# Seven whole tiles in the ring of expert weights, four turns an expert, and a router in another order

## The reference, cut to what matters

```python
logits = t @ w_router                                # 256 tokens x 8 experts
top_vals, top_idx = lax.top_k(logits, 2)
gates = softmax(top_vals)
for e in range(8):                                   # w_gate, w_up: 1024 x 3584; w_down: 3584 x 1024
    he = (silu(t @ w_gate[e]) * (t @ w_up[e])) @ w_down[e]
    out = out + combine[:, e:e + 1] * he             # combine holds the gates of the chosen experts
...
return rmsnorm(h, final_norm)
```

## Time and profile before

| | us |
|---|---|
| median of 3 runs (2175.14 to 2179.47) | 2176.42 |
| the profiled execution | 2182.77 |
| its span, first to last instruction | 2180.7 |
| TensorE busy | 2114.9 (97%) |
| VectorE, ScalarE, GpSimd busy | 837.9, 465.8, 24.7 |
| moved by DMA | 534.35 MB, mean 245 GB/s |

### The profile page before, as it was taken

How to read it: one execution, slowest core, us unless ns; L and a number is a source line. 1 busy time by engine, 2 the same in 40 slices (tenths; PEclk the granted TensorE clock), 3 DMA queues, 4 the chain that set the end, 5 groups by cost and what they waited for, 6 DMA issues and landing times.

```text
span 2180.7 us, 67375 instructions
## 1 busy us (share of the span) xinstructions
PE 2114.9 (97%) x30418; PEld 1945.7 (89%) x30418; DVE 837.9 (38%) x2085; ACT 465.8 (21%) x1074; POOL 24.7 (1%) x43
## 2 busy tenths in 40 slices
PE   9999999999999999999997899999999999999998
PEld 8889999856999986899986789999999999999997
DVE  4357676314766655467759520101010101010102
ACT  3432112113311134211023221111111111111112
POOL 1000000000000000000000000000000000000000
PEclk9999999999999999999998999999999999999999
DMA  9241444240334423324431338999999999999997
GB/s 394 93 173 72 162 174 175 81 169 8 139 150 169 160 97 136 155 117 174 168 142 40 116 117 327 413 416 410 418 410 418 409 418 409 418 417 416 418 417 287
DMA packets 78407, 534.35 MB, mean 245 GB/s; under 512 B 9106, under 2 KB 9235, under 8 KB 41939
## 3 DMA queue, kind: packets, MB, share of 16 engines
q1 hardware_dynamic: 74450, 519.82, 59.3%
q0 software_dynamic: 3840, 12.85, 1.6%
HBM read 523.00 MB, written 9.63 MB: 244 GB/s over the span
## 4 chain that ended last, share of the span: by engine, by line
PE 65%; DMA 4%; DVE 2%; ACT 1%; issue 1%; DVEq 0%; SPq 0%; ACTq 0%
PE ps L1866 24%; PE ps L1224 12%; PE ps L1882 11%; PE ps L1266 7%; DMA slot<-in_w_moe 4%; PE ps L1141 4%; PE ps L1633 2%; PE ps L1616 1%; DVE scr L2549 0%; PE ps L1813 0%; PE ps L1157 0%; PE ps L1503 0%; PE ps L1489 0%; PE ps L1096 0%; PE ps L1570 0%
## 5 line engine op out<-in xcount | busy, mean ns | idle before, releaser
L1866 PE MATMUL ps<-scr,slot 128*64 128x88 f32 x14336 | 595.4, 241 | 11.1 <-issue 5.4
L1866 PEld LDWEIGHTS ps<-scr,slot 128*64 128x64 f32 x14336 | 562.8, 137 | 22.1 <-issue 12.4
L2698 DVE TENSOR_TENSOR scr<-scr,ps 128x88 f32<-128x88 f32 x224 | 55.1, 246 | 727.1 <-ACT scr L982 727.1
L1882 PE MATMUL ps<-scr,slot 128*64 128x88 f32 x7168 | 315.5, 239 | 1.9 <-issue 1.9
L1882 PEld LDWEIGHTS ps<-scr,slot 128*64 128x64 f32 x7168 | 292.0, 137 | 5.1 <-issue 5.1
L1266 PE MATMUL ps<-scr,slot 128*128 128x256 f32 x1056 | 237.6, 380 | 1.6 <-DVE scr L2369 1.6
L1266 PEld LDWEIGHTS ps<-scr,slot 128*128 128x128 f32 x1056 | 196.6, 191 | 26.0 <-DVE scr L2369 2.0
L982 ACT ACTIVATE scr<-ps 128x88 f32<-128x88 f32 x224 | 54.5, 243 | 743.8 <-PE ps L1866 743.8
L1224 PE MATMUL ps<-vtok,slot 128*128 128x128 f32 x1056 | 139.6, 275 | 0.0
L1224 PEld LDWEIGHTS ps<-vtok,slot 128*128 128x128 f32 x1056 | 128.8, 192 | 0.2
L1224 PE MATMUL ps<-vtok,proj 128*128 128x128 f32 x1056 | 128.7, 275 | 0.0
(11 more groups left out here) (412 smaller groups left out, 2058.4 us busy)
## 6 DMA issues: line engine op xcount, KB each, us to landing
slot<-in_w_moe SPq DMA_DIRECT2D x224, 1024.0 KB, 12.2
slot<-in_w_moe SPq DMA_DIRECT2D x224, 512.0 KB, 12.2
slot<-in_w_ffn SPq DMA_DIRECT2D x33, 3072.0 KB, 10.8
slot<-in_w_even_in SPq DMA_DIRECT2D x3, 3072.0 KB, 27.2
slot<-in_w_odd_qk SPq DMA_DIRECT2D x2, 3072.0 KB, 10.6
slot<-in_w_s_glu SPq DMA_DIRECT2D x2, 3072.0 KB, 11.9
slot<-in_w_odd_v SPq DMA_DIRECT2D x2, 2048.0 KB, 8.4
slot<-in_w_even_in SPq DMA_DIRECT2D x2, 1536.0 KB, 10.6
```

What stands on the lines that cost most here:

```text
L1866: m = pe.matmul(gate_up(j, k)[s:s + STRIP], w[:, o:o + STRIP], xg[:, c], start=c == 0, stop=c == KD - 1, skip_group_check=True)
L1882: m = pe.matmul(y_sum(d)[s:s + STRIP], w[:, o:o + STRIP], hid[j][:, 0:CAP], start=False, stop=False, skip_group_check=True)
L2698: dve.tensor_tensor(hid[f % 4][:, 0:CAP], gbuf[f % 4][:, 0:CAP], gate_up(f, 1), ALU.mult).then_inc(hid_ready, 1)
```

## The change

`RING` becomes 7 and an expert is `TURNS` = 4 turns of seven tiles. The ring takes tiles 0 to 6 as well: places of 12 KB a partition, two to a slot, so three and a half slots. A tile is one transfer of 1.5 MB, issued when its place's last `down` is done; the early issue of the up part is gone. `hrow`, `xl` and `returned` move to other tensors. The seventh tile of a turn has its gate and up sums in bank 6, the others in banks 4 and 5 as before. TensorE's experts 0 to 6 are one loop with their change inside (so `turn_rows` is run once more, on one row loaded in addition), and the last expert has a loop of three turns and one turn written out. `hrow` is made after tiles 7 and 8 and waits for no place. In the router the products for the final gain come after the counts, four products that fill time (`busy`, bank 5) stand in their old place, ScalarE does the exponent of the gates before the two copies, and TensorE waits for those copies at the first change of expert. The branch for crowded experts changes likewise and isn't shown.

```diff
@@ -41,8 +41,9 @@
 UP, DOWN = 2 * D, D
-RING = 4
-GROUPS = FE_TILES // RING
+RING = 7
+TURNS = FE_TILES // RING
+ROUNDS = EXPERTS * TURNS
 WEIGHTED_AT = 16
@@ -262,7 +263,9 @@
 def gate_up(f, k):
-    return ps[:, 4 + f % 2, k * CAP:(k + 1) * CAP]
+    if f % RING == RING - 1:
+        return ps[:, 6, k * CAP:(k + 1) * CAP]
+    return ps[:, 4 + f % RING % 2, k * CAP:(k + 1) * CAP]
 small_loaded, late_loaded = sem("small_loaded"), sem("late_loaded")
@@ -312,8 +315,7 @@
 combined, first_copied = sem("combined"), sem("first_copied")
-moe_up_loaded = [sem(f"moe_up_loaded{i}") for i in range(RING)]
-moe_down_loaded = [sem(f"moe_down_loaded{i}") for i in range(RING)]
+moe_loaded = [sem(f"moe_loaded{i}") for i in range(RING)]
 moe_free = sem("moe_free")
@@ -427,24 +429,16 @@
 mix0 = {"even_out": 0, "odd_out": KD, "mla_o": 2 * KD}
-lead_slots, ring_slots = ([(len(LOADED) - SLOTS + k) % SLOTS for k in some]
-                          for some in ((0, 1), (2, 3)))
-def up_places(two):
-    return [slots[two[h // 3]][:, h % 3 * UP:(h % 3 + 1) * UP] for h in range(RING)]
-def down_places(two):
-    return [slots[two[1]][:, UP + h * DOWN:UP + (h + 1) * DOWN] for h in range(RING)]
-lead_loaded = [_n[k] + 16 * n for k, n in zip(lead_slots, (3, 1 + RING))]
-lead_ups, lead_downs = up_places(lead_slots), down_places(lead_slots)
-ups, downs = up_places(ring_slots), down_places(ring_slots)
-lead = [slots[k] for k in lead_slots]
-hrow = lead[0][:, 0:2 * D].rearrange("p (g d) -> p g d", g=2)
-xl = lead[0][0:CAP, 2 * D:3 * D]
-returned = lead[1][:, 0:4 * D].rearrange("p (n d) -> p n d", n=4)
+tile_slots = [(len(LOADED) - SLOTS + h // 2) % SLOTS for h in range(RING)]
+places = [slots[s][:, h % 2 * (UP + DOWN):(h % 2 + 1) * (UP + DOWN)]
+          for h, s in enumerate(tile_slots)]
+ups, downs = [x[:, 0:UP] for x in places], [x[:, UP:UP + DOWN] for x in places]
+hrow = proj[:, 8:16].rearrange("p a n -> p (a n)").rearrange("p (g d) -> p g d", g=2)
+xl = proj[0:CAP, 16:20].rearrange("p a n -> p (a n)")
+returned = [yT[:, 4:8].rearrange("p a n -> p (a n)"),
+            xbp[:].rearrange("p a n -> p (a n)")[:, 0:D],
+            rgw[:].rearrange("p k j n -> p (k j n)"), part(34, 4)]
 where = part(25)[:, 16:64].rearrange("p (n c) -> p n c", c=8)
@@ -493,43 +487,17 @@
     return SLOTS + max(n for n in range(len(LOADED)) if n % SLOTS == s) + 1
-def load_up(h, unit):
-    sp.dma_start(ups[h], a["w_moe"][bass.ds(unit, 1), :, 0:UP].rearrange(
-                     "o p n -> p (o n)")).then_inc(moe_up_loaded[h], 16)
-def load_down(h, unit):
-    sp.dma_start(downs[h], a["w_moe"][bass.ds(unit, 1), :, UP:UP + DOWN].rearrange(
-                     "o p n -> p (o n)")).then_inc(moe_down_loaded[h], 16)
+def load_tile(h, unit):
+    sp.dma_start(places[h], a["w_moe"][bass.ds(unit, 1), :, :].rearrange(
+                     "o p n -> p (o n)")).then_inc(moe_loaded[h], 16)
 for h in range(RING):
-    for s in lead_slots[0:1 if h < 3 else 2]:
-        sp.wait_ge(slot_free, left(s))
-    sp.dma_start(lead_ups[h], a["w_moe"][h, :, 0:UP]
-                 ).then_inc(slot_loaded[lead_slots[h // 3]], 16)
-for h in range(RING):
-    sp.dma_start(lead_downs[h], a["w_moe"][h, :, UP:UP + DOWN]
-                 ).then_inc(slot_loaded[lead_slots[1]], 16)
-for h in range(RING):
-    for s in ring_slots[0:1 if h < 3 else 2]:
-        sp.wait_ge(slot_free, left(s))
-    load_up(h, RING + h)
-for h in range(RING):
-    load_down(h, RING + h)
-last = EXPERTS * FE_TILES // RING - 1
-sp.wait_ge(up_ready, 2 * (FT0["moe"] + RING) + 2)
-load_up(0, 2 * RING)
-with sp.Fori(2, last) as i:
+    sp.wait_ge(slot_free, left(tile_slots[h]))
+    load_tile(h, h)
+with sp.Fori(1, ROUNDS) as i:
     for h in range(RING):
-        sp.wait_ge(up_ready, i * (2 * RING) + (2 * (FT0["moe"] + h - RING) + 4))
-        load_up((h + 1) % RING, i * RING + (h + 1))
         sp.wait_ge(moe_free, i * RING + h + 1)
-        load_down(h, i * RING + h)
-for h in range(RING):
-    if h + 1 < RING:
-        sp.wait_ge(up_ready, 2 * (FT0["moe"] + (last - 1) * RING + h) + 4)
-        load_up(h + 1, last * RING + h + 1)
-    sp.wait_ge(moe_free, last * RING + h + 1)
-    load_down(h, last * RING + h)
+        load_tile(h, i * RING + h)
 for g in range(2):
@@ -564,11 +532,12 @@
         pool.wait_ge(mo["loaded"], 16 * (e - 2))
-    pool.dma_start(xl, rows_in[e * T:e * T + CAP, :]).then_inc(mo["loaded"], 16)
+    n = CAP if e < EXPERTS else 1
+    at_ = min(e, EXPERTS - 1) * T
+    pool.dma_start(xl[0:n], rows_in[at_:at_ + n, :]).then_inc(mo["loaded"], 16)
 pool.wait_ge(mo["scattered"], ZEROED)
 pool.wait_ge(mo["rows"], 3)
-pool.wait_ge(moe_free, RING + RING)
 for n in range(4):
@@ -584,7 +553,7 @@
     pool.indirect_dma_start(
-        out=returned[:, n], out_offset=None, in_=rows_out,
+        out=returned[n], out_offset=None, in_=rows_out,
         in_offset=bass.IndirectOffsetOnAxis(ap=back_row[:, n:n + 1], axis=0)
@@ -1010,13 +979,13 @@
     take_tokens(1)
+    act.wait_ge(rt["diff"], 2)
+    act.activation(tiny[:, GA:GA + 1, 0:2], tiny[:, GA:GA + 1, 0:2], ACT.Exp
+                   ).then_inc(rt["exp"], 1)
     for b in range(2):
...
                        ).then_inc(fin["rowtaken"], 1)
-    act.wait_ge(rt["diff"], 2)
-    act.activation(tiny[:, GA:GA + 1, 0:2], tiny[:, GA:GA + 1, 0:2], ACT.Exp
-                   ).then_inc(rt["exp"], 1)
 def final_norm():
@@ -1707,12 +1676,7 @@
     pe.wait_ge(tile_taken, TILE0["s5_glu"] + 2 * KD)
-    for c in range(KD):
-        m = pe.matmul(ps[:, 6 + c // 4, c % 4 * P:c % 4 * P + P],
-                      v("final_norm", c).to_broadcast([P, P]), ident, start=True, stop=True,
-                      skip_group_check=True)
-        if c % 4 == 3:
-            m.then_inc(fin["row"], 1)
+    busy(4, 5)
     pe.wait_ge(mo["sel"], 2)
@@ -1722,27 +1686,18 @@
               skip_group_check=True).then_inc(mo["pos"], 1)
-def up_weights(e, f, first):
-    if first and f < RING:
-        pe.wait_ge(slot_loaded[lead_slots[f // 3]], lead_loaded[f // 3])
-        return lead_ups[f]
-    pe.wait_ge(moe_up_loaded[f % RING], e * (16 * GROUPS) + 16 * (f // RING))
-    return ups[f % RING]
-def down_weights(e, f, first):
-    if first and f < RING:
-        pe.wait_ge(slot_loaded[lead_slots[1]], lead_loaded[1])
-        return lead_downs[f]
-    pe.wait_ge(moe_down_loaded[f % RING], e * (16 * GROUPS) + 16 * (f // RING))
-    return downs[f % RING]
+    for c in range(KD):
+        m = pe.matmul(ps[:, 6 + c // 4, c % 4 * P:c % 4 * P + P],
+                      v("final_norm", c).to_broadcast([P, P]), ident, start=True, stop=True,
+                      skip_group_check=True)
+        if c % 4 == 3:
+            m.then_inc(fin["row"], 1)
 def experts_dense():
...
     pe.wait_ge(rt["comb"], 2)
+    pe.wait_ge(fin["rowtaken"], 2)
     for e in range(EXPERTS):
@@ -1852,11 +1801,7 @@
 def up(j, loads, inputs=None):
-    if loads is None:
-        pe.wait_ge(slot_loaded[lead_slots[j // 3]], lead_loaded[j // 3])
-    else:
-        pe.wait_ge(moe_up_loaded[j], loads)
-    w = lead_ups[j] if loads is None else ups[j]
+    pe.wait_ge(moe_loaded[j], loads)
     for k in range(2):
@@ -1864,38 +1809,32 @@
                 m = pe.matmul(gate_up(j, k)[s:s + STRIP],
-                              w[:, o:o + STRIP], xg[:, c], start=c == 0,
+                              ups[j][:, o:o + STRIP], xg[:, c], start=c == 0,
                               stop=c == KD - 1, skip_group_check=True)
         m.then_inc(up_ready, 1)
-def down(j, loads, hids):
-    if loads is None:
-        pe.wait_ge(slot_loaded[lead_slots[1]], lead_loaded[1])
-    else:
-        pe.wait_ge(moe_down_loaded[j], loads)
-    w = lead_downs[j] if loads is None else downs[j]
+def down(j, hids):
     pe.wait_ge(hid_ready, hids)
...
             o = d * P + s
-            m = pe.matmul(y_sum(d)[s:s + STRIP], w[:, o:o + STRIP],
-                          hid[j][:, 0:CAP], start=False, stop=False,
+            m = pe.matmul(y_sum(d)[s:s + STRIP], downs[j][:, o:o + STRIP],
+                          hid[j % 4][:, 0:CAP], start=False, stop=False,
                           skip_group_check=True)
     m.then_inc(moe_free, 1)
-def four(e, i, last=False, first=False):
+def seven(e, i, last=False):
     def at(scale, plus):
-        return e * (GROUPS * scale) + i * scale + plus
-    here = None if first else at(16, 0)
+        return e * (TURNS * scale) + i * scale + plus
     for j in range(RING):
-        if j < RING - 1:
-            up(j + 1, here)
+        if j + 1 < RING:
+            up(j + 1, at(16, 16))
         elif not last:
-            up(0, at(16, 16), at(2, 3))
-        down(j, here, at(RING, FT0["moe"] + j + 1))
+            up(0, at(16, 32), at(2, 3))
+        down(j, at(RING, FT0["moe"] + j + 1))
 def open_sums(copies):
@@ -1907,28 +1846,19 @@
 gather(1)
-up(0, None, 1)
+up(0, 16, 1)
 open_sums(None)
-four(0, 0, first=True)
-with pe.Fori(1, GROUPS) as i:
-    four(0, i)
-turn_rows(16)
-open_sums(2)
-turn_sums(2)
```

(21 more changed lines are left out.)

28 lines of the change are left out of this document (12 added, 16 removed).

## The result

The changed kernel takes 2162.12 us (median of 6 runs, 2160.93 to 2167.64); the kernel before took 2179.6 us in the same comparison. The ratio is 0.9928, 95% interval 0.9917 to 0.994: 0.7% faster, where 0.9% was forecast (2156.6 / 2176.42 = 0.9909). The profiled execution took 2164.06 us, span 2162.1, against 2182.77 and 2180.7.

The account below looks back on a forecast made before the run. The weight stream, 3% slower than TensorE, was taken to bound the kernel before. Afterwards TensorE's 2131.7 + 14 of code = 2145.7, against the stream's 2143.7, plus 2 gave 2147.7 instead of 2167.5: median 2156.6 us, range 2148 to 2172.

Parts of the forecast that it names:

- Start of stream: Ring's first load after the prefetch: asked for when tile 0 is free at 1302.2, bytes from 1303.3 instead of 1315.6.
- Router: Gain-row products moved behind the counts fill TensorE's gap and keep its clock: -2.7 us, bounds +0.3 to -2.7.
- Price of a tile's transfer: Weight stream with 12 KB rows: 427 GB/s, 3.68 us a tile instead of 3.763; 217 tiles, plus 32.9 us for rows.
- TensorE's bill: TensorE's own work from the first up products on, without any stall: 836.4 us, ending at 2131.7.
- Code: TensorE's instruction-fetch stalls at entries of new code, about 1.0 us a packet: 14 us, bounds 8 and 18.
- Rival C: Experts' loop no longer stays in TensorE's instruction store and is fetched anew: 30 to 150 us against the forecast, chance 0.12.
- for two close chains: End of the experts: TensorE's chain (2145.7) and the stream's (2143.7) hinder one another, 2 us added to the later.
- The median: Whole kernel: profiled execution 2163.0 us, less the 6.35 it stood over the median before, gives 2156.6, 0.9% less.
- B: Weight transfers: row size buys nothing, the stream alone binds at 3.763 us a tile: 2170.6 us, chance 0.18.
- E: First turn's stalls and a clock fall after one push back the seven early loads: within 0.2%, 2172 to 2180, chance 0.05.
- D: Code costs 8 us and transfers run at 433 GB/s: 2148.6 us, chance 0.09.

Follow-up runs that it names:

- `late_start`: The changed kernel, but SyncE issues the ring's first load only when tile 3 is used up, not tile 0: 2168.81 us, 0.9954 of the kernel before.
- `third_of_bytes`: The changed kernel, but from the eighth tile on only each tile's down third is loaded, so the result isn't computed: 2144.46 us, 0.9837 of the kernel before.
- `two_transfers`: The changed kernel, but each tile comes as two transfers of 8 and 4 KB a partition: 2174.74 us, 0.9983 of the kernel before.
- `old_router`: The changed kernel, but gain-row products stand ahead of the wait for `sel` again, without the four filler products: 2164.08 us, 0.9933 of the kernel before.

## Why the prediction was right, and where it was off

**Start of stream.** Right: forecast 1303.3 with up(0) at 1295.3, so 8.0 us after it; measured 1301.9 with 1293.9, also 8.0. That it mattered is `late_start`'s 7.2 us.

**Router.** Right: -2.7 forecast, -2.8 measured between count and up(0), the clock at 1.00; the other 1.3 us by which up(0) came early are variation ahead of it.

**Price of a tile's transfer.** Right, 3.68 forecast, 3.690 measured. The whole stream: 2137.7 - 1301.9 = 835.8 us = 217 x 3.690 + 35.1, where 32.9 stood for the rows.

**TensorE's bill.** Right: 836.4 us without stalls, and `third_of_bytes` shows 836.9 with 0.9 us of code stalls in its last expert.

**Code.** Right in kind, 14 us forecast. The price of a packet rested on 13 packets; TensorE's queue brought 16 from 1315 to 2167 in the kernel before, which makes it 0.5 to 1.1 us, not 0.6 to 1.3. Measured by the length of turns against undisturbed ones: 3.0 in the first two turns of expert 0 (26.25 and 27.15 against 24.95 and 25.48), 7.3 at the last expert's loop, 1.1 in its last turn (27.91 to the start of its last product, against 26.75 in `third_of_bytes`, which fetched there too), none at the loop's tail: 11.4. The last turn was oversized (4 us); its packets came mostly when the stream was ebbing. Its counterpart, the entry of the last expert's loop, was undersized (5 us). Rival C's chance was fair: the body with its change is 5.7 packets long, and 7.2 was already too much.

**The step that failed** is the 2 us added "for two close chains", after comparing the two sums at the end. Stretch by stretch they don't run side by side. In experts 1 to 5 there are no code stalls and the transfers bind (up to 106.6 against 104.7 us an expert, 7.6 us in all over experts 1 to 6 by `third_of_bytes`); in experts 0 and 7 there are code stalls and TensorE binds. Both are paid: 836.9 + 7.6 + 2.9 + 7.7 = 855.1. The term measured 7.6, not 2. What saved the sum was luck, in that the code was smaller by 2.6 and up(0) earlier by 1.4: 2147.7 forecast for the last down product, 2149.0 measured.

**The median.** The profiled execution was forecast at 2163.0 and took 2164.06. It stood 1.9 us over its median, though, where the one of before stood 6.35 over its own; carrying that offset over unchanged is 4.4 of the 5.5 us between 2156.6 and 2162.12.

**Rivals.** B fell to `two_transfers`, E to the start of the stream, though a fall of the clock after the first turn's stalls, as E has it, did come in `old_router`. C did not occur, but its mechanism is shown. D's transfers (433 GB/s) didn't come.

## What to carry to other kernels

When two engines' totals are close, compare them stretch by stretch and add up the larger of each stretch: the end pays for every stretch's own limit. A loop's body with everything that its outer loop adds, and with the parts of blocks at both its ends, has to fit TensorE's store; here 5.7 packets did, and 7.2, for which nine packets came, brought all of them back in every pass, at 1.0 to 1.6 us each. After a change that unties a buffer from a queue, look at which transfers can now move into a stretch where the DMA engines idle: that gave more here (7.3 us) than removing all of the last expert's code stalls (1.3 us, not shown in the medians).

## What the runs showed of the hardware

- TensorE kept a loop 6.9 packets of 16 KB long; one of 7.2 brought nine an expert; 8.4 brought ten a turn and 10.8 twelve a pass. A store of eight packets fits all four.
- A code packet's price depends on the stream beside it: the same entry cost 7.3 us under a full stream (4.6 to 10.0 in other runs) and 0.9 with the DMA engines at a share of 0.56.
- Rows of 12 KB move at 426 GB/s, 8 and 4 KB mixed at 418, both with the DMA engines at a share of 1.01 to 1.02; a packet of 12 KB took 464 ns, one of 8 and one of 4 KB 477 together.
- TensorE can be held back by transfers and be recorded as busy for 65.00 of 65 us: 1700 products against 1721, and 1720 under the same full stream with the input rows left out.
